# Two encoder layers with 32 experts each: the experts' TensorE order, the place of layer 1's row loads, and the place of its modulation bias loads

## The reference, cut to what matters

```python
for l in range(DEPTH):                                   # DEPTH = 2
    mod = (c_act @ ada_w[l] + ada_b[l])[:, None, :]
    sh1, sc1, g1, sh2, sc2, g2 = jnp.split(mod, 6, axis=-1)
    h = rms_norm(x, ln1_g[l]) * (1.0 + sc1) + sh1
    cols = h @ w_in[l]                                   # 512 rows, split into a, b, c, d
    ...                                                  # three attentions, one long convolution (d)
    x = x + g1 * (mix @ w_out[l])
    h = rms_norm(x, ln2_g[l]) * (1.0 + sc2) + sh2
    x = x + g2 * hier_moe(h, ...)                        # each row goes to 2 of 32 experts
# one expert: (silu(xe @ w_gate[e]) * (xe @ w_up[e])) @ w_down[e], 1024 -> 256 -> 1024, f32
# long convolution: the filters are made by a small network, then transformed (cosine and sine sums)
```

## Time and profile before

| what | value |
|---|---|
| median of 3 runs | 1513.91 us (1513.27 to 1514.66) |
| the profiled execution | 1513.77 us, its span 1511.4 us |
| TensorE busy | 1326.7 us, 88% |
| VectorE, ScalarE, GpSimd busy | 40%, 24%, 18% |
| mean granted TensorE clock | 0.958 |
| layer 0's experts | about 503 to 770 us |
| layer 1's experts | about 1228 to 1490 us |

### The profile page before, as it was taken

The page is one execution under the profiler, slowest core; times in us unless marked ns, Lnnn a source line. Parts: engine busy times, 40 slices in busy tenths (PEclk is TensorE's granted clock), DMA queues, the critical chain, the costliest instruction groups (busy, mean ns, idle before and its releaser), DMA issues.

```text
span 1511.4 us, 18434 instructions
## 1 busy us (share of the span) xinstructions
PE 1326.7 (88%) x6928; PEld 767.9 (51%) x6928; DVE 597.8 (40%) x1314; ACT 357.1 (24%) x791; POOL 268.0 (18%) x283
## 2 busy tenths in 40 slices
PE   5899899988998898888998999999889969997883
PEld 1446546655745554444444565566464545554441
DVE  5635522357716321433154251435782541221112
ACT  1411022545402111111202211244551211111111
POOL 0201200000100353322221030000010015333222
PEclk8999999999999799999987999999999979999997
DMA  8801220555494799999943112135307489999984
GB/s 288 318 16 56 101 84 12 215 191 180 133 361 166 293 327 379 410 404 404 358 170 118 56 58 70 58 133 202 112 1 297 160 299 387 400 400 403 402 343 147
DMA packets 100228, 336.83 MB, mean 223 GB/s; under 512 B 29988, under 2 KB 34724, under 8 KB 74890
## 3 DMA queue, kind: packets, MB, share of 16 engines
q1 hardware_dynamic: 74600, 305.52, 52.1%
q0 software_dynamic: 15072, 16.85, 5.0%
q10 hardware_dynamic: 10468, 13.28, 2.5%
HBM read 324.13 MB, written 29.00 MB: 234 GB/s over the span
## 4 chain that ended last, share of the span: by engine, by line
PE 77%; DVE 12%; ACT 4%; issue 4%; DMA 1%; POOL 1%; SPq 0%; DVEq 0%; POOLq 0%; ACTq 0%
PE bank L504 71%; PE bank L785 3%; PE bank L896 2%; DVE pr_r L2145 2%; ACT pr_r L1502 2%; DVE ht_r L2005 1%; DVE pr_r L2148 1%; PE bank L622 1%; DMA big<-in_ada_w_dram 1%; DVE mix_r L2019 1%; DVE big L1736 1%; DVE small L2003 0%; DMA x_tok<-x_rows 0%; DVE big L1923 0%; DVE ht_r L1989 0%
## 5 line engine op out<-in xcount | busy, mean ns | idle before, releaser
L504 PE MATMUL bank<-big,pr_r 128*64 128x256 f32 (+2 forms) x3032 | 426.3, 400 | 43.8 <-DVE pr_r L2148 22.6
L504 PEld LDWEIGHTS bank<-big,pr_r 128*64 128x64 f32 (+1 forms) x3032 | 258.3, 152 | 181.7 <-issue 93.6
L504 PE MATMUL bank<-big,ht_r 128*128 128x512 f32 (+3 forms) x832 | 309.1, 555 | 1.9 <-ACT ht_r L1455 1.9
L504 PEld LDWEIGHTS bank<-big,ht_r 128*128 128x128 f32 (+1 forms) x832 | 143.5, 189 | 133.0 <-issue 121.5
L504 PE MATMUL bank<-big 128*128 128x256 f32 (+4 forms) x496 | 169.4, 480 | 22.5 <-DVE big L1930 5.9
L1651 POOL DMA_INDIRECT x_rows<-ht_r,slot_i x64 | 102.0, 1594 | 321.4 <-DVE ht_r L2151 302.8
L504 PEld LDWEIGHTS bank<-big 128*128 128x128 f32 (+2 forms) x496 | 92.4, 198 | 67.2 <-issue 29.8
L1502 ACT ACTIVATE pr_r<-bank 64x256 f32<-64x256 f32 x64 | 24.1, 377 | 403.4 <-PE bank L504 403.4
L2145 DVE TENSOR_TENSOR pr_r<-pr_r,bank 64x256 f32<-64x256 f32 x65 | 27.5, 423 | 219.6 <-ACT pr_r L1502 214.6
L2151 DVE SCALAR_TENSOR_TENSOR ht_r<-bank,mix_r,mod 128x512 f32<-128x512 f32 x65 | 48.8, 751 | 132.6 <-PE bank L504 132.6
L504 PE MATMUL bank<-ht_r,big 128*128 128x512 f32 x192 | 85.4, 607 | 1.4 <-ACT ht_r L1341 1.4
(11 more groups left out here) (299 smaller groups left out, 1237.5 us busy)
## 6 DMA issues: line engine op xcount, KB each, us to landing
big<-in_moe_w_gate_dram SPq DMA_DIRECT2D x59, 1024.0 KB, 17.8
big<-in_moe_w_up_dram SPq DMA_DIRECT2D x59, 1024.0 KB, 22.3
big<-in_moe_w_down_dram SPq DMA_DIRECT2D x59, 1024.0 KB, 26.3
big<-in_ada_w_dram SPq DMA_DIRECT2D x16, 3072.0 KB, 11.3
big<-in_w_in_dram SPq DMA_DIRECT2D x4, 3072.0 KB, 13.6
big<-in_w_out_dram SPq DMA_DIRECT2D x4, 2048.0 KB, 9.3
mod<-in_ada_b_dram SPq DMA_DIRECT2D x12, 512.0 KB, 10.4
x_tok<-in_moe_w_gate_dram SPq DMA_DIRECT2D x6, 1024.0 KB, 17.0
```

The costliest lines, as they stand in the source:

```text
L504: return nc.tensor.matmul(o, l, r, start=start, stop=stop)
```

## The change

There are three parts. **Experts:** the rows of expert e+2, not e+1, are transposed in `expert(e)`; k = 0 of the next expert's `gate_up` goes ahead of `act_transpose(e)`, k = 1 ahead of `down(e)`. `begin(e + 1)` holds the waits of the next expert, that for its weights among them. GpSimd's loop is as it was. **Rows:** layer 1's row tiles go into `mix_r` (tiles 0 to 2) and the place of `ln1` (tile 3), behind `m21`; the sine sums go behind the columns d, as in layer 0; `x_tok` gets the rows again later, behind the load of the columns c. **Bias rows:** `load_mods` and `next_parts` are issued behind the loads of expert 31.

```diff
@@ names of the buffers
+        row_at = lambda l, t: x_tok[:, t, :] if l == 0 else ln1 if t == NT - 1 else at(mix_r, t * D, D)
...
-        s_b_of = (f_tmp, s_b)
-        f_even_of, f_odd_of = (ar(11264, S), f_even), (ar(11264 + S, S), f_odd)
+        s_b_of = (f_tmp, ar(17920, S))
+        f_even_of, f_odd_of = (ar(11264, S),) * 2, (ar(11264 + S, S),) * 2
@@ TensorE, start of a layer
                 else:
                     filter_cos(1)
-                    filter_sin(0)
-                    filter_sin(1)
                     transpose_rows(0)
...
-                if l == 0:
-                    filter_sin(0)
-                    filter_sin(1)
+                filter_sin(0)
+                filter_sin(1)
                 project("a", range(1))
@@ TensorE, experts
-                def gate_up(b, s):
+                def gate_up(b, s, ks=range(KT)):
                     wg, wu, _ = expert_slot(s)
-                    for k in range(KT):
+                    for k in ks:
...
-                def expert(e):
-                    b, s = e % 2, EXPERT_SLOTS[l][e]
+                def x_turn(e):
+
+                    pe.wait_ge(gathered[e % 4], NE // 4 * 16 * l + 16 * (e // 4 + 1))
+                    if e >= 2:
+                        pe.wait_ge(xt_ready, NE * l + e - 1)
+                    pe.sem_inc(waited, 1)
+                    x_transpose(e % 2, e % 4).then_inc(xt_done, 1)
+
+                def begin(e):
+
+                    s = EXPERT_SLOTS[l][e]
                     pe.wait_ge(xt_ready, NE * l + e + 1)
                     pe.wait_ge(slot_full[s], expert_full(e, l))
                     if e >= 2:
                         pe.wait_ge(acth_ready, NE * l + e - 1)
-                    gate_up(b, s).then_inc(gu_done, 1)
+                    gate_up(e % 2, s, range(1))
+
+                def expert(e):
+                    b, s = e % 2, EXPERT_SLOTS[l][e]
+                    gate_up(b, s, range(2 if e else 1, KT)).then_inc(gu_done, 1)
                     if e == 0:
                         pe.wait_ge(code_ready, l + 1)
                         nc.tensor.transpose(bank[7][0:1, 0:P], o_code[:, 0:1], ident[:, :]).then_inc(over_turned, 1)
+                        x_turn(1)
+                    if e + 2 < NE:
+                        x_turn(e + 2)
                     if e + 1 < NE:
-                        pe.wait_ge(gathered[(e + 1) % 4], NE // 4 * 16 * l + 16 * ((e + 1) // 4 + 1))
-                        if e >= 1:
-                            pe.wait_ge(xt_ready, NE * l + e)
-                        pe.sem_inc(waited, 1)
-                        x_transpose(1 - b, (e + 1) % 4).then_inc(xt_done, 1)
+                        begin(e + 1)
                     pe.wait_ge(acth_ready, NE * l + e + 1)
...
                     act_transpose(b).then_inc(at_done, 1)
+                    if e + 1 < NE:
+                        gate_up(1 - b, EXPERT_SLOTS[l][e + 1], range(1, 2))
                     pe.wait_ge(actT_ready, NE * l + e + 1)
@@ SyncE: behind the load of layer 1's columns "c"
+                    if l and c == IN[3]:
+                        done(sp, "fdo1")
+                        for t in range(NT):
+                            sp.dma_start(x_tok[:, t, :], x_rows[t * P:(t + 1) * P, :]).then_inc(x_back, 16)
@@ SyncE: after expert 11 before, after expert 31 now
                         load_bias(l + 1)
-                        load_mods(l + 1)
-                        sp.wait_ge(ada_stored, 16 * 3)
-                        for c in range(3):
-                            sp.dma_start(next_parts[c], ada_rows[c].rearrange("(g r) n -> g r n", r=32)[:, 0]).then_inc(parts_in, 16)
-
+
+                if l + 1 < DEPTH:
+                    load_mods(l + 1)
+                    sp.wait_ge(ada_stored, 16 * 3)
+                    for c in range(3):
+                        sp.dma_start(next_parts[c], ada_rows[c].rearrange("(g r) n -> g r n", r=32)[:, 0]).then_inc(parts_in, 16)
@@ SyncE: layer 1's rows
+                if l + 1 < DEPTH:
+                    done(sp, "m21")
                 for t in range(NT):
-                    if l + 1 < DEPTH:
-                        done(sp, "fco1" if t < 2 else "fdo1")
-                    sp.dma_start(x_tok[:, t, :], x_rows[t * P:(t + 1) * P, :]).then_inc(x_in[t], 16)
+                    if l + 1 < DEPTH and t == NT - 1:
+                        sp.wait_ge(gsc1_ready, l + 1)
+                    sp.dma_start(row_at(1, t) if l + 1 < DEPTH else x_tok[:, t, :], x_rows[t * P:(t + 1) * P, :]).then_inc(x_in[t], 16)
@@ ScalarE, experts
-                    if e + 1 < NE:
-                        act.wait_ge(xt_done, NE * l + e + 2)
-                        x_evac(1 - b).then_inc(xt_ready, 1)
+                    for n in ((1, 2) if e == 0 else (e + 2,)):
+                        if n < NE:
+                            act.wait_ge(xt_done, NE * l + n + 1)
+                            x_evac(n % 2).then_inc(xt_ready, 1)
@@ VectorE, start of a layer
                 else:
-                    filter_evac("c")
-                    filter_evac("d")
                     rows(0, gsc1, sh1)
                     rows(1, gsc1, sh1)
...
-                    filter_evac("c")
+                filter_evac("c")
...
-                if l == 0:
-                    filter_evac("d")
+                filter_evac("d")
...
+                        if l and half + t == 0:
+                            v.wait_ge(x_back, 16 * NT)
```

More of the change, by code:

```diff
@@ L303, in trunk @@
             sem("ov_" + n) for n in "w i2 x xt gu sil act at aT y yv t".split())
+        gsc1_ready, x_back = sem("gsc1_ready"), sem("x_back")
         x_stored, gate_ready, pairw_ready = (sem(n) for n in "x_stored gate_ready pairw_ready".split())
@@ L967, in next_filter @@
                     return last
-                pe.wait_ge(gathered[0], NE // 4 * 16 * l + 16)
-                pe.sem_inc(waited, 1)
-                x_transpose(0, 0).then_inc(xt_done, 1)
+                x_turn(0)
+                begin(0)
                 for e in range(NE):
@@ L1334, in layer @@
                         act.wait_ge(nss_ready, 2 * NT * l + t)
-                    A_(sq_junk, x_tok[:, t, :], ACT.Square,
+                    A_(sq_junk, row_at(l, t), ACT.Square,
                        accum_out=nss[:, t:t + 1]).then_inc(nss_ready, 1)
@@ L1771, in layer @@
                         mod_take(c)
-                    step(TT(gsc1, gsc1, ln1, ALU.mult))
+                    TT(gsc1, gsc1, ln1, ALU.mult).then_inc(gsc1_ready, 1)
+                    v.wait_ge(gsc1_ready, l)
                 win = lambda t: window[:, t].unsqueeze(1).to_broadcast([P, 2, CH])
@@ L1777, in scaled @@
                 def scaled(n, gsc):
-                    step(TT(h_tok[:, n % 2, :], x_tok[:, n % NT, :], gsc, ALU.mult))
+                    step(TT(h_tok[:, n % 2, :], row_at(l if n < NT else 0, n % NT), gsc, ALU.mult))
                 def shifted(n, sh):
@@ L2175, in next_filter @@
                     else:
-                        nc.vector.tensor_copy(s_b, b[:, :]).then_inc(job_taken_v, 1)
+                        nc.vector.tensor_copy(s_b_of[l + 1], b[:, :]).then_inc(job_taken_v, 1)
                 def over_list(r):
```

## The result

The changed kernel takes 1562.4 us (median of four runs, 1558.07 to 1572.21), the kernel before beside it 1513.59 (1512.09 to 1514.66): a ratio of 1.0335, 95% interval 1.0291 to 1.0378. It is slower, as predicted, but by 49 us and not by 17; the range ended at 1548. The profiled execution is the slowest of the four, 1572.21 us.

What follows compares the result with a forecast made beforehand. TensorE or the weight loads bound the experts before; afterwards the gather loop would. Layer 0's 0.7 + 5.9 and layer 1's 5.2 + 11.8, less 7 at the join, gave +16.6 us, so 1531 us; range 1505 to 1548.

Steps and rivals of the forecast that it cites:

- the loop: Experts' stages: waiting for gathers makes a loop over two experts of 16.53 us, with a stand of 3.3 us.
- I take half a fall, 0.85 us a turn: Experts' stages: clock falls behind gather stands, half of 1.69 us each, cost 5.9 us in layer 0, 11.8 in layer 1.
- each stand costs a fall: Rival, experts' stages: every stand costs the whole 1.69 us, 11.8 and 23.7 us, join only 4.5 less: 1551 us; chance 0.08.
- to expert 31's there are 242.8 us in layer 1: Layer 1's experts before the change, the base from which the loop was to cost 5.2 us more.
- the join: Between the layers: earlier row loads and moved sine products save 7 us, 4.5 as the poor end.
- the 2.5 us for a fuller clock: Join: the columns d may take 41.47 us, not 43.95, as TensorE stands less before them.
- the bias rows at nothing: Layer 0: moving 2 MB of loads behind load 31 buys nothing with the gather loop as bound, and costs nothing.
- bias rows or waves land late: Rival, join: late landings take away its gain, seven us more, 1538 us; chance 0.04.
- The gaining rivals: Experts' stages: gathers land sooner, 1506 us, chance 0.15; or short landings throughout, 1501 us, chance 0.09.
- The estimate of 2.6 us: Landing time of a 256 KB gather by the skill's page; by it no wait for gathers arises.

Runs made afterwards that it cites:

- e9: The changed kernel with sixteen extra identity transposes ahead of each wait for a gather, in layer 1 alone: 1549.1 us, ratio 1.0242.
- e1: The kernel before with the new experts' order alone, rows at the join and bias rows as before: 1567.7 us, ratio 1.0333.
- e7: The kernel before with the join's rows part alone, experts' order and bias rows as before: 1506.7 us, ratio 0.9948.
- e2: The change without the experts' order, so the join's rows part and the bias rows' part on the kernel before: 1509.8 us, ratio 0.9960.
- e10: The kernel before with the bias rows' loads alone moved behind the last expert's loads: 1512.8 us, ratio 0.9999.
- e3: The changed kernel with gather(e+4) issued one turn earlier, ahead of scatter(e) on GpSimd: 1516.1 us, ratio 0.9995.
- e14: e7 with the eight scatters of the slot table issued ahead of expert 0's scatter: 1505.9 us, ratio 0.9960.
- e11: e3 with the next weights' wait behind the down pass and the bias rows in the middle of layer 0's loads again: 1510.0 us, ratio 0.9982.

## Why the prediction was right and wrong

**Right: the loop.** The stands are where they were forecast, at line 881, released by a gather, in nearly every second expert. With the slow work counted at its full-speed length, the loop has the predicted length: in layer 1 a pair of full-speed turns is 13.1 us, fourteen of these and a last of 12.6 are 196.0, and the stands sum to 53.0 (51.6 of them for gathers, 16 stands of 3.2; forecast were 3.3): 249.0 us against the 248.0 that I had. The landings moved little, 9.2 us for 8.9.

**Wrong: "I take half a fall, 0.85 us a turn".** This is the term that failed. The number of falls was right, 14 in layer 1 and 7 in layer 0; their price was not. I had priced a fall by the gate pass alone, 1.69 us; the rows above give 2.9, since the transposes, k = 0 and the down pass are slow too. And I had halved it, as partly slept through; but of 75.1 us at half clock in layer 1 only 6.1 lie in stands. 278.1 less 249.0 leaves 29.1 us in layer 1, 2.1 a fall, where I had 11.8. In layer 0 work and stands are 196.0 and 34.0 us, against fifteen pairs of 14.3 and 9 us of further stands before, the filter pieces alike in both (17 of the experts have one, not the 15 of the description above): 6.5 us more. Of 18.5 that leaves 12.0, 1.7 a fall, where I had 5.9. That is 23 us of the profile's miss, counted; e9 shows its kind, as layer 1 came down 19 us (12 from e1's) when TensorE kept at work. The rival "each stand costs a fall", with 1.69 us each, had nearly the right price.

**Wrong: "to expert 31's there are 242.8 us in layer 1".** That included the block behind expert 31. From the true 233.9 the loop alone costs 15.1 us and not 5.2; the slip is 8.9 us of it. In layer 0 the loop without falls cost 6.5 us where I had 0.7. I had spread one pace over both halves of it: with its falls, the stretch from expert 1 to 15 took 26.3 us more than before, where the loads had been no bound, and that from 15 to 31, with most filter pieces, 7.8 less.

| term, us | forecast | profile | miss |
|---|---|---|---|
| falls, both layers | 17.7 | 41.1 | 23.4 |
| loop, layer 1 | 5.2 | 15.1 | 9.9 |
| loop, layer 0 | 0.7 | 6.5 | 5.8 |
| join | -7.0 | -8.2 | -1.2 |
| elsewhere | 0 | 4.0 | 4.0 |
| sum | 16.6 | 58.5 | 41.9 |

These are the numbers of the profiled run, the slowest of four. The median is 9.8 us below it; e1's profile, with the same loop, shows 37.0 and 12.4 us in the layers where this one shows 44.2 and 18.5.

**Right: the join,** -7 forecast, -8.2 measured, but the closeness is luck: two terms missed in opposite ways. The columns d took 43.67 us, so the 2.5 us for a fuller clock did not come (in e7 they did: 41.47 us at a mean clock of 1.00). And the columns started 14.8 us nearer, not 11.6: the spread took 7.4 us and not 9.0, the rows' stage 8.7 and not 10.0. **Right here only: the bias rows at nothing.** No stand at the waves in the changed kernel, where the loop binds and the waves landed 8.4 us after SyncE asked for them; where loads bind, 7 us of stand (e2, e10), as "bias rows or waves land late" had it.

**The gaining rivals** were wrong for a reason that I had not seen. With landings out of the way (e3) I had 1506 or 1501; it is 1516 beside a kernel before of 1517. The gathers landed in 9.2 us under the loads' traffic. The estimate of 2.6 us that follows from the Trainium skill, page "DMA: Bandwidth & Descriptors", section "Anatomy of one DMA — SWDGE (gpsimd) path", was not seen there.

**The clock rule.** In the changed kernel's layer 1 each of the 14 stands of 2.0 us and more has a fall in it or behind it. The Trainium skill, page "TensorE: Matmul & The Clock Gate", section "HAM oscillation — how this bites in real kernels", says this of a loop that waits for a DMA in each turn, and this trace agrees, 14 of 14; by that rule I had 1551, the nearest of my cases. The stands of 3.27 and 3.14 us in e10 and e14 had none behind them.

**Open.** What e3 would take with a full clock; and why only some stands of 2 to 3.3 us have a fall behind them. Why e11's join keeps 2.8 us less than e7's is on record in part: its columns d took 43.71 us at a mean clock of 0.95, e7's 41.47 at 1.00; why the clock differed there is not shown.

## What to carry to other kernels

When work is pulled ahead in one engine's order, move the issue of what feeds it by as much; check this before counting the stands that the new order fills. Price a stand as its own length plus the slow work behind it, all of it up to the next thing that the loop waits for. And look whether a faster turn can be used: against loads that bound the stage it made the stands longer, and TensorE's clock lower.

## What the runs showed of the hardware

- Behind stands of 2.26, 3.17 and 3.35 us TensorE's clock was at half; behind stands of 1.21 us (e9), 2.08, 3.14 (e14) and 3.27 us (e10) it was not. The two falls worked out from rows cost 2.6 and 2.9 us of work; over all falls of the changed kernel it is 2.1 us each in layer 1 and 1.7 in layer 0.
- Most of the time at half clock came with the work behind a stand: 69.0 of 75.1 us in layer 1. The clock can fall within a stand too (mean 0.77 over one of 4.75 us).
- Eight or sixteen useless transposes ahead of a wait, 1.1 and 2.0 us, made layer 1 15 and 19 us shorter than in the changed kernel's profile, 8 and 12 than in e1's.
- The gathers' landing was 9.2 us at the median, 8.9 before, though the DMA share of 1340 to 1420 us fell from 1.03 before to 0.94.
